# VectorE takes three of the four low parts of a streamed weight chunk during expert routing, GpSimd one instead of two

## The reference

```python
q = (xc @ wq).reshape(PEER_CHUNK, PEER_HEADS, 2, half)
sc = jnp.einsum('chpd,hpnd->chpn', q, sub_keys)       # 128 key scores, twice per head
s1, i1 = lax.top_k(sc[:, :, 0], PEER_TOPK)            # 16 best of each half
s2, i2 = lax.top_k(sc[:, :, 1], PEER_TOPK)
cand = (s1[..., :, None] + s2[..., None, :])          # 16 x 16 candidates
cidx = (i1[..., :, None] * PEER_NKEYS + i2[..., None, :])
top_s, pos = lax.top_k(cand, PEER_TOPK)               # 16 best candidates
eidx = jnp.take_along_axis(cidx, pos, axis=-1)
g = jax.nn.softmax(top_s, axis=-1)
a = jax.nn.gelu(einsum(u[eidx], xc))                  # expert activations
out = einsum(g * a, v[eidx])
```

## Time and profile before

| | us |
|---|---|
| median of 3 runs (2502.34 to 2509.07) | 2506.39 |
| the profiled execution's own time | 2505.94 |
| its span, first to last instruction | 2504.1 |
| PE busy | 2412.5 (96%) |
| DVE busy | 1748.9 (70%) |
| ACT busy | 1343.7 (54%) |
| POOL busy | 709.0 (28%) |

### The profile page before, as it was taken

One profiled execution on the slowest core, in us unless ns is written; L12 is line 12 of the kernel. 1 busy time (PEld: TensorE's weight loads), 2 busy tenths in 40 slices (PEclk: granted clock), 3 DMA queues, 4 the chain that ended last, 5 costly groups with the idle time before them and its releaser, 6 DMA issues. The chain is left out here.

```text
span 2504.1 us, 57329 instructions
## 1 busy us (share of the span) xinstructions
PE 2412.5 (96%) x16509; PEld 2211.3 (88%) x16509; DVE 1748.9 (70%) x3945; ACT 1343.7 (54%) x2396; POOL 709.0 (28%) x564
## 2 busy tenths in 40 slices
PE   6999999999999999999999999999999999899998
PEld 6899999999888888889999999988888887688996
DVE  5647777887677777554777788777777767556346
ACT  3545555776555555454555567655555543444443
POOL 5665444000000000566544400000000043134665
PEclk9999999999999999999999999999999999999999
DMA  6244566444566666623466644456666644333554
GB/s 239 85 153 168 210 230 226 168 152 180 177 245 236 246 236 243 237 85 137 167 217 225 228 164 161 174 182 241 241 241 242 243 157 158 142 135 110 174 186 152
DMA packets 98053, 475.31 MB, mean 190 GB/s; under 512 B 11808, under 2 KB 13344, under 8 KB 50720
## 3 DMA queue, kind: packets, MB, share of 16 engines
q1 hardware_dynamic: 97392, 472.91, 53.3%
q10 hardware_dynamic: 560, 1.19, 0.1%
HBM read 438.41 MB, written 35.65 MB: 189 GB/s over the span
## 5 line engine op out<-in xcount | busy, mean ns | idle before, releaser
L1415 ACT ACTIVATE wh<-ring 128x512 fp32r<-128x512 f32 x1428 | 881.9, 627 | 613.9 <-ACTq L1414 609.3
L2103 DVE TENSOR_TENSOR wl<-ring,wh 128x512 fp32r<-128x512 f32 x961 | 674.1, 707 | 273.0 <-DVEq L2102 254.2
L1100 PE MATMUL PS<-xh,wh 128*128 128x256 f32 x2048 | 593.6, 290 | 9.7 <-PEq L1096 8.2
L1100 PE MATMUL PS<-xl,wh 128*128 128x256 f32 x2048 | 579.6, 283 | 0.0
L1100 PE MATMUL PS<-xh,wl 128*128 128x256 f32 x2048 | 579.5, 283 | 0.0
L510 POOL TENSOR_TENSOR wl<-ring,wh 128x512 fp32r<-128x512 f32 x295 | 390.8, 1349 | 289.1 <-POOLq L509 287.3
L895 PE MATMUL PS<-wh,xh 128*128 128x512 f32 x1088 | 425.2, 391 | 2.5 <-PEq L892 2.5
L895 PE MATMUL PS<-wh,xl 128*128 128x512 f32 x1088 | 423.5, 389 | 0.0
L895 PE MATMUL PS<-wl,xh 128*128 128x512 f32 x1088 | 423.3, 389 | 0.0
L1100 PEld LDWEIGHTS PS<-xh,wh 128*128 128x128 f32 x2048 | 392.3, 192 | 15.3 <-issue 14.6
L1100 PEld LDWEIGHTS PS<-xl,wh 128*128 128x128 f32 x2048 | 392.9, 192 | 0.0
(11 more groups left out here) (339 smaller groups left out, 3826.5 us busy)
## 6 DMA issues: line engine op xcount, KB each, us to landing
ring<-in_peer_u SPq DMA_DIRECT2D x128, 1024.0 KB, 4.8
ring<-in_peer_v SPq DMA_DIRECT2D x128, 1024.0 KB, 4.8
acts<-stg SPq DMA_DIRECT2D x124, 256.0 KB, 2.1
gains<-acts SPq DMA_DIRECT2D x124, 256.0 KB, 4.9
ring<-in_w_in SPq DMA_DIRECT2D x24, 1024.0 KB, 4.9
ring<-in_w_gate_up SPq DMA_DIRECT2D x22, 1024.0 KB, 4.8
ring<-in_peer_wq SPq DMA_DIRECT2D x16, 1024.0 KB, 4.8
ring<-in_w_down SPq DMA_DIRECT2D x11, 1024.0 KB, 4.9
```

Source lines behind the costliest of these rows:

```text
L1100: last = pe.matmul(PS[:, 2 * j, 0:S], w[:, q, k * P:(k + 1) * P], x[:, at, :], start=at + i == 0, stop=at + i == 9)
L1415: act.activation(wh[:, q, :], ring[:, s, q * QW:(q + 1) * QW], ACT.Copy).then_inc(high_ready[q], 1)
L2103: part = dve.tensor_tensor(wl[:, q, :], ring[:, s, q * QW:(q + 1) * QW], wh[:, q, :].bitcast(F32), SUB)
```

## The change

In the 36 chunks of the routing, POOL makes part 0 alone, and waits for the end of it before it signals. DVE makes parts 1, 2 and 3. In the heads loop DVE issues each low part behind the last instruction of a step and ahead of the wait for that step's end: the step's last instruction itself signals `dve_own` (`mark`), then comes the low part (`low_next`), then the wait (`settle`). The `engine_nop` instructions go. `low_next` signals `parts_ready[q]` for part 3 too directly from the instruction. DVE's increment of `chunk_free` is no longer part of the low part: `freed(k)` stands behind a later `settle()`.

```diff
 # POOL, per chunk
-                        for q in (0, 2):
-                            pool.wait_ge(high_ready[q], 1)
-                            pool.sem_inc(high_ready[q], -1)
-                            pool.tensor_tensor(wl[:, q, :], ring[:, s, q * QW:(q + 1) * QW],
-                                               wh[:, q, :].bitcast(F32), SUB).then_inc(
-                                                   parts_ready[q] if q == 0 else pool_own, 1)
-                        pool.wait_ge(pool_own, 1)
-                        pool.sem_inc(pool_own, -1)
-                        pool.sem_inc(parts_ready[2], 1)
+                        pool.wait_ge(high_ready[0], 1)
+                        pool.sem_inc(high_ready[0], -1)
+                        own(pool.tensor_tensor(wl[:, 0, :], ring[:, s, 0:QW], wh[:, 0, :].bitcast(F32), SUB))
+                        pool.sem_inc(parts_ready[0], 1)
                         pool.sem_inc(chunk_free[s], 1)
 # DVE
+                def low_next(k):
+                    s, q = k // 3 % 2, k % 3 + 1
+                    dve.wait_ge(high_ready[q], 1)
+                    dve.sem_inc(high_ready[q], -1)
+                    dve.tensor_tensor(wl[:, q, :], ring[:, s, q * QW:(q + 1) * QW], wh[:, q, :].bitcast(F32),
+                                      SUB).then_inc(parts_ready[q], 1)
+                def freed(k):
+                    dve.sem_inc(chunk_free[k // 3 % 2], 1)
 # heads loop, first half
-                    own(dve.engine_nop())
-                    best(0, cand)
-                    low_odd(0)
+                    mark(last)
+                    low_next(0)
+                    settle()
+                    mark(best(0, cand))
+                    low_next(1)
+                    settle()
                     ...
-                    own(dve.engine_nop())
-                    low_odd(1)
-                    best(8, candr)
+                    mark(last)
+                    low_next(2)
+                    settle()
+                    mark(best(8, candr))
+                    low_next(3)
+                    settle()
+                    freed(2)
                     ...
+                    mark(last)
+                    low_next(4)
+                    settle()
                     ...
+                    mark(dve.tensor_scalar(pj[:, 1, :], p16[:, :], 15, None, ALU.bitwise_and))
+                    low_next(5)
+                    settle()
+                    mark(dve.tensor_copy(pf[:, :, :], pj[:, :, :]))
+                    shifted(0)
+                    shifted(1)
+                    settle()
+                    freed(5)
 # heads loop, second half
+                    mark(is_one(0))
+                    low_next(6)
+                    settle()
+                    mark(pick(0))
+                    low_next(7)
+                    settle()
+                    mark(picked(0))
+                    low_next(8)
+                    settle()
+                    mark(is_one(1))
+                    low_next(9)
+                    settle()
+                    freed(8)
+                    mark(pick(1))
+                    low_next(10)
+                    settle()
+                    mark(picked(1))
+                    settle()
+                    low(1, 3)
```

More of the change, by code:

```diff
@@ L2373, in _, with mark, settle, best_keys @@
                 halves_low_xT()
-                def best_keys(c, s, beside=None):
+                def mark(ins):
+                    ins.then_inc(dve_own, 1)
+                def settle():
+                    dve.wait_ge(dve_own, 1)
+                    dve.sem_inc(dve_own, -1)
+                def low_next(k):
[6 more added lines that the diff above has]
+                    dve.sem_inc(chunk_free[k // 3 % 2], 1)
+                def best_keys(c, s, lows=False):
                     dve.wait_ge(scores_ready, 1)
@@ L2405, in _ @@
                         best_keys(2 * i + s, s)
-                def low_odd(k):
-                    low(k // 2 % 2, 2 * (k % 2) + 1)
                 dve.wait_ge(pool_lows_done, 1)
                 dve.sem_inc(pool_lows_done, -1)
-                best_keys(N_WQ - 2, 0, low_odd)
-                best_keys(N_WQ - 1, 1, low_odd)
+                best_keys(N_WQ - 2, 0, True)
+                best_keys(N_WQ - 1, 1, True)
                 with dve.Fori(0, PH) as c:
@@ L2418, in is_one @@
                     def is_one(a):
-                        own(dve.tensor_tensor(oneh[:, :, :], bc(iota16[:, :].unsqueeze(1), TT * TOPK, TOPK),
-                                              bc(pf[:, a, :].unsqueeze(2), TT * TOPK, TOPK), ALU.is_equal))
+                        return dve.tensor_tensor(oneh[:, :, :], bc(iota16[:, :].unsqueeze(1), TT * TOPK, TOPK),
+                                                 bc(pf[:, a, :].unsqueeze(2), TT * TOPK, TOPK), ALU.is_equal)
                     def pick(a):
@@ L2446, in _ @@
                         dve.max_index(p16[:, k:k + 8], t16[:, k:k + 8], cand[:, t, :])
-                        dve.match_replace(candr[:, t, :], t16[:, k:k + 8], cand[:, t, :], -3e38)
-                    own(dve.engine_nop())
-                    low_odd(1)
-                    best(8, candr)
+                        last = dve.match_replace(candr[:, t, :], t16[:, k:k + 8], cand[:, t, :], -3e38)
+                    mark(last)
+                    low_next(2)
+                    settle()
+                    mark(best(8, candr))
@@ L2451, in _ @@
+                    low_next(3)
+                    settle()
+                    freed(2)
                     for t in range(TT):
                         k = TOPK * t + 8
-                        dve.max_index(p16[:, k:k + 8], t16[:, k:k + 8], candr[:, t, :])
-                    own(dve.engine_nop())
-                    low_odd(2)
+                        last = dve.max_index(p16[:, k:k + 8], t16[:, k:k + 8], candr[:, t, :])
+                    mark(last)
+                    low_next(4)
```

50 lines of the change are left out of this document (26 added, 24 removed).

## The result

| | before | after |
|---|---|---|
| median, us (4 runs each, 3 of the ones of before shown above) | 2507.59 | 2531.21 (2529.33 to 2532.45) |
| ratio to before, 95% interval | | 1.0097 (1.0085 to 1.0109) |
| span of the profiled execution | 2504.1 | 2527.3 |
| POOL busy, page | 709.0 | 596.6 |
| DVE busy, page | 1748.9 | 1752.0 |

What follows compares the result with a forecast made beforehand. PE was taken as the bound, busy nearly everywhere, with the slot's return just critical. Late slots and the first chunk, less today's gaps, gave 30.8 us for two routings, plus 1.5 for the clock: 2539 us, range 2514 to 2550.

Steps and rivals of the forecast that it cites:

- The slot's return: Heads loop: c0's and c2's slots return behind the next chunk's part 1, loads issue at 5.5 and 5.15, PE needs 4.13.
- The walk through an iteration: Heads loop: DVE and POOL operations block each other, c2 starts 1.3 late, the next c0 1.0; iteration 25.3 us.
- the walk's clean case: Heads loop, everything on time: c1's part 1 starts at T + 4.45 after ACT, load issued at T + 4.8, 0.65 to 0.7 late.
- clean lateness only: Rival, chance 0.20: slots come back at T + 4.8 and no collision adds to it; 2523 us.
- The part taken off POOL: Routing: 36 low parts of 1.3 us leave POOL per routing; worth nothing by itself, since nobody waits for POOL's idle time.
- the forecast loss at part 2 of the same chunk: First chunk of a routing: part 2, now behind the indices, ends about 227.4 where PE needs it at 226.4; 1.1 us lost.
- The sum: Per routing: late slots 20.7 less 0.6, plus 1.1, less 5.8 lost today: 15.4; both routings 30.8, plus 1.5.
- the allowance for the clock: Second routing, which starts at the low clock: 1.5 us more, since a new stall may keep it there.
- The marks cover the waits: DVE's low parts beside waits cost 0.61 each; rival that they don't, at 0.26 + 0.69: 2567 us, chance 0.04.
- The clock doesn't fall at the new gaps: PE: new stalls are about 1 us in 12; rival that the clock falls: 2557 us or more, chance 0.04.
- The rival in which the gaps close: Increment takes effect in time, POOL holds DVE half as often, DVE's waits are covered; 2497 us, chance 0.04.
- The quicker load: Rival, chance 0.06: a load not issued beside a save takes 4.4 to 4.5 us; 2502 to 2506, no change.

Runs made afterwards that it cites:

- e1_nop: The changed kernel, with the slots of c0 and c2 handed back by an engine_nop right behind that chunk's part 3; 2494.93 us, ratio 0.9961 to the kernel before.
- e2_before_late: The kernel before, with only DVE's hand-back of c0's and c2's slots moved behind part 1 of the next chunk; 2555.95 us, ratio 1.0203.
- e9_spaced: The changed kernel, with c1's slot handed back 0.6 to 0.9 us later, still ahead of part 1 of c2; 2528.95 us, ratio 1.0098.
- e6_split2: e1_nop with the old split: POOL makes parts 0 and 2, DVE parts 1 and 3; 2498.53 us, ratio 0.9973 to the kernel before.
- e8_pool_nop: e1_nop, with POOL too signalling parts_ready from its instruction and handing the slot back by an engine_nop; 2491.90 us, ratio 0.9947 to the kernel before.
- e7_three_late: The changed kernel, with c1's slot also handed back late, behind part 1 of c2; 2570.77 us, ratio 1.0265 to the kernel before.
- e5_before_nop: The kernel before, its split and order kept; DVE's low parts signal from the instruction, an engine_nop behind part 3 hands back the slot; 2504.96 us, ratio 1.0003.

## Why the prediction was right, point by point

**The slot's return.** Right, and shown from both sides: e1_nop takes it out (-36 us against the changed kernel), e2_before_late puts it in alone (+49). The loads for even chunks from 4 on are issued 4.8 to 5.9 us after the start of the chunk that had the slot, 5.07 in the mean, forecast 5.5 and 5.15. In the iteration shown a pair costs 25.39 - 23.04 = 2.35 us, in the median of all sixteen 2.2, forecast 2.3.

**The walk through an iteration.** Its sum was right, its reason was not. The prediction set the hand-back by a collision: POOL's part 0 of the next chunk would hold DVE's part 3 of c0, and the one-hot of c2, and part 1 of the next chunk would come at 5.15 and 4.8 us. In the iteration shown neither is held. Part 1 of c1 starts at 4.68 (353.81); part 3 of c0 had started at 352.17, before POOL's part:

```profile
353.05 1.29 POOL L635 TENSOR_TENSOR wl<-ring,wh 128x512 fp32r<-128x512 f32 x1 [4.19 <-POOLq L634]
```

Part 1 of c1 waits for ACT, as in the walk's clean case (4.45), plus 0.23, since ACT's part 0 of c1 is itself late (352.24). In c2 the one-hot runs before POOL's part (365.80) comes, and part 1 of c3 waits for ACT, which is through with it at 366.42:

```profile
364.41 0.68 DVE L2440 TENSOR_TENSOR arena<-iota,pf 128x512 f32<-128x512 f32 x1
366.56 1.10 DVE L2382 TENSOR_TENSOR wl<-ring,wh 128x512 fp32r<-128x512 f32 x1 [1.47 <-DVEq L2381]
```

It is so nearly everywhere: of the 36 late hand-backs of both routings, 34 have DVE's part 1 start 0.14 or 0.15 us behind the end of ACT's, and only two come later by 0.6 and 0.9, behind a part 3 that ran beside POOL's part. One of the two, DVE's row and POOL's:

```profile
428.25 1.69 DVE L2382 TENSOR_TENSOR wl<-ring,wh 128x512 fp32r<-128x512 f32 x1
```

```profile
428.10 1.29 POOL L635 TENSOR_TENSOR wl<-ring,wh 128x512 fp32r<-128x512 f32 x1 [3.15 <-POOLq L634]
```

What makes ACT late beyond the clean case is the load for the odd chunk, which takes long; in e9_spaced, where the loads for c3 are quick, the next hand-back comes at the clean 4.83 in the median and at 5.2 at most. The rows of the loads issued at 341.49 and 345.48, the last number being us to landing:

```profile
ring<-in_peer_u SPq DMA_DIRECT2D x1, 1024.0 KB, 5.0
```

```profile
ring<-in_peer_u SPq DMA_DIRECT2D x1, 1024.0 KB, 6.6
```

So c2 starts at 361.74, which is c0's start plus 12.61: 4.68 + 0.39 + 5.19 + 2.35. The forecast had 12.9. The 2.35 answers to the 2.24 of before; the wait that part 0 now has for its own end was put at 0.15 and came at 0.11.

So the mechanism that ran was that of the rival *clean lateness only*, the wait for ACT, with a cost on top that the prediction did not have. The clean case put an even chunk 0.65 to 0.7 late; it was 1.1 in the mean. Of the difference 0.27 is the later issue (5.07 instead of 4.8), mostly by the slow loads for odd chunks, and the rest is the way from the issue to PE, 7.56 instead of 7.39. The measured 2531 lies midway between that rival's 2523 and the forecast's 2539. That the collision's price (1.3 and 1.0) came so near to what the slow loads cost is luck.

**The part taken off POOL** was said to be worth nothing. Not quite: at the first chunk of the routing the copy of `best_keys` was held by POOL's second part, 1.33 us where it now takes 0.20:

```profile
220.82 1.33 DVE L2399 COPY arena<-s16c 128x64 f32 x1 [0.27 <-DVEq L1855]
```

```profile
220.29 0.20 DVE L2420 COPY arena<-s16c 128x64 f32 x1 [0.26 <-DVEq L2375]
```

The first of the two is the kernel before. So the wait of the first chunk's part 1, which the prediction called immovable at 2.4, fell to 0.8; in e6_split2, with POOL's second part again, it is back at 1.95 summed. Against it stands the forecast loss at part 2 of the same chunk: 1.1 expected, 1.25 measured (1.18 and the refill of PE's pipeline behind it).

**The sum.** The stretch of 37 chunks grew by 14.15 in the first routing (221.37 to 235.52; forecast 15.4) and by 12.8 in the second (221.83 to 234.61; forecast 15.4 and the 1.5 for the clock): 26.9 in all, where 32.3 stood. In the first, the late slots cost 19.0 where 20.1 stood, chiefly because the load of chunk 36 came with a gap of 0.3 and had been counted like any other; the first chunk's part 1 cost 1.6 less; 1.1 us of gaps at other places, which no term had, and 0.15 more at part 2 came back. In the second the allowance for the clock was wrong altogether. PE had lost 1.5 us there to the low clock; after, it waits less for its part 1 (1.0 instead of 2.95) and has the full clock from its first chunk on, although it idles again at part 2:

```profile
1230.00:1234.00 4.00, 2.98 (x23) 2.59 (x22) 2.98 (x18) 3.38 (x7) 1.27 (x1) 1.00 0.03 10
1234.00:1238.00 4.00, 2.20 (x17) 1.92 (x16) 4.00 (x21) 1.86 (x2) 1.30 (x1) 1.00 0.01 2
```

The shorter wait (2.0), the clock (1.5) and the unused allowance (1.5) are 5.0 below the forecast, and the late slots are 2.2 below it (17.9); 1.4 us of other gaps and of part 2 came back, and some 1.6 because the kernel before had lost that much less in the rest of this routing than in the first. That the shorter wait is why the clock stayed up is not shown: in the second routing of e8_pool_nop and e9_spaced the same part waited for 2.5 and 2.4 us, and the clock was 1.00 there too. The remaining 3.7 between 26.9 and the spans' 23.2 lie outside the routings, 0.3 ahead of the first, 1.6 between the two and 1.9 behind the second. There the change touches only the waits of `best_keys` for the earlier key scores, and behind the second routing nothing; the profiled executions of all kernels differ there as much or more: 775.4 to 778.2 us between the routings and 1060.0 to 1069.3 behind the second.

**DVE does not become the bound**: right, e1_nop has three low parts on it and no gap. **The marks cover the waits**: right, low parts behind a step start without idle time. **The clock doesn't fall at the new gaps**: right, 1.00 in the window of the first routing. **The busy times**: POOL's fell by 112 us, forecast 95. DVE's rose by 3, forecast 20 to 40, although it makes 72 more low parts; it is held less by POOL (the TENSOR_SCALAR behind the positions takes 0.17 us in the iteration above where it took 1.27), and how the rest adds up was not followed.

**The rival in which the gaps close** had its mechanism right (fewer blocks, covered waits) and e1_nop is its number, 2494.9 against the 2497 given there; only the placement of two increments stood between it and the changed kernel. The 2497 had kept a wait of 2.4 at the first chunk that fell, so a part of that agreement is chance. **The quicker load** was wrong in sign: in the changed kernel the loads for odd chunks took 4.9 to 7.3 from chunk 3 on. The Trainium skill, "DMA: Bandwidth & Descriptors", section "Anatomy of one DMA", whose fit for the other issuing path gave the estimate of 4.4, has no run here near it; the shortest load took 4.6. With the 358 GB/s that the same page of the Trainium skill gives as the limit of the memory side (section "Where 436 GB/s comes from") the same fit would be an estimate of 4.9. The loads of 4.7 to 5.2 below agree with that sum but not with the limit in it: the busiest stretches of 2 us in the first routing moved 416 GB/s before and 422 after.

## What to carry to other kernels

Where a buffer is handed back from an engine's instruction stream, ask what the stream can be made to wait for between the last use of the buffer and the increment. An increment behind a wait for the *next* buffer's data closes a ring of load, use and hand-back, and the double buffer is gone for that step; in e1_nop an `engine_nop` behind the last use carried the increment, and the stream had nothing to wait for. Check in the trace that the hand-back then comes behind the end of the last use, as it did there (0.26 us). And before trusting a gain from covered waits, compute from the trace the latest time at which a load may be issued. In the kernel before the load for c0 had no room left, while the one for c2, issued 3.4 us after the start of the chunk that had the slot, had 0.9 of the 4.28.

## What the runs showed of the hardware that was not expected

A 1 MB load issued 3.3 to 4.4 us behind the one before it, with a 256 KB save mostly about 2 us ahead of it, took 5.3 to 7.3 us in 120 of 152 cases; one issued 4.5 us or more behind took 5.2 or less in 603 of 640, and 5.7 at most (chunks 2 to 37 of both routings in the eleven profiled executions). Distance alone is not the rule: in e7_three_late, of the fourteen loads in the heads loop 3.97 behind, with the save 3.04 ahead, eight took 4.7 to 5.2 and six 5.4 to 7.0, and in e2_before_late those at 3.3 to 3.4 took 5.0 to 5.4. Bytes don't explain it either: load, save and load are 2.25 MB, an estimate of 5.7 us at the 416 GB/s above, while from the first issue to the second landing go some 10.4 (4.0 and 6.4). What does is open.

A subtraction on DVE that comes while POOL's runs is held for the rest of POOL's 1.3 us, and time saved on DVE ahead of it can be spent there: in e5_before_nop the 0.3 us per chunk taken out of DVE's stream bought nothing. It isn't only subtractions: the copy of 128 x 64 took 1.33 us beside POOL's part and 0.20 without, the TENSOR_SCALAR of 128 x 32 1.27 and 0.17.
